# A hybrid attention block on one core: attention units spread over three scheduling periods instead of two

## What is computed

```python
h = modulate(x, g_mix, shift, scale)                 # rmsnorm, then adaLN
proj = h @ w_in                                      # q, k, v of 8 + 8 heads, a gate, forget logits
# stick-breaking heads (8), strict causal
log_beta = log_sigmoid(z); log_keep = where(strict, log_beta - z, 0)
suffix = cumsum(log_keep, reverse=True) - log_keep   # over the keys
w = where(strict, exp(log_beta + suffix), 0);  o_sb = w @ v
# forgetting heads (8), causal; q and k are rms-normed first
z = q @ k.T * scale + f_q - f_keys;  o_fx = softmax(z) @ v
o_sb = rmsnorm(o_sb); o_fx = rmsnorm(o_fx) * sigmoid(gate)
x = x + gate1 * (concat(o_sb, o_fx) @ w_out)
```

## Time and profile before

| | |
|---|---|
| median of 3 runs | 1144.94 us (1144.14 to 1145.12) |
| profiled execution | 1145.88 us |
| its span, first to last instruction | 1144.1 us |
| granted TensorE clock, mean | 0.996 |
| PE busy | 1108.5 us, 97% of the span |
| DVE busy | 596.1 us, 52% |
| ACT busy | 446.4 us, 39% |
| periods 0 to 39 | from 442.9 us to about 725 us of the span |

### The profile page before, as it was taken

The page is one execution under the profiler, slowest core; times in us unless marked ns, Lnnn a source line. Parts: engine busy times, 40 slices in busy tenths (PEclk is TensorE's granted clock), DMA queues, the critical chain, the costliest instruction groups (busy, mean ns, idle before and its releaser), DMA issues.

```text
span 1144.1 us, 14298 instructions
## 1 busy us (share of the span) xinstructions
PE 1108.5 (97%) x5142; PEld 885.2 (77%) x5142; DVE 596.1 (52%) x829; ACT 446.4 (39%) x693; POOL 71.7 (6%) x68
## 2 busy tenths in 40 slices
PE   8999999999999999889999999999999999999997
PEld 5788888888788868678778767778888888878876
DVE  3746464655644556777766677663333333434343
ACT  5522222222222235566776665353222222312312
POOL 1000000000000001000000000000000000225350
PEclk9999999999999999999999999999999999999999
DMA  9755675565573631221212211332333333223221
GB/s 343 212 148 165 195 207 166 165 190 165 166 227 105 193 92 47 80 67 44 73 52 66 65 47 42 89 91 74 92 97 96 97 94 92 74 83 98 96 92 74
DMA packets 169687, 133.32 MB, mean 117 GB/s; under 512 B 5436, under 2 KB 150956, under 8 KB 169644
## 3 DMA queue, kind: packets, MB, share of 16 engines
q1 hardware_dynamic: 168704, 130.60, 38.0%
q0 software_dynamic: 768, 2.10, 0.8%
q10 hardware_dynamic: 172, 0.06, 0.0%
HBM read 128.54 MB, written 2.10 MB: 114 GB/s over the span
## 4 chain that ended last, share of the span: by engine, by line
PE 76%; DVE 12%; ACT 7%; issue 3%; DMA 1%; SPq 0%; DVEq 0%; ACTq 0%
PE bank L694 24%; PE bank L696 24%; PE bank L695 24%; DVE w_lo L1471 2%; DVE tmp_b L1867 2%; DVE pt_lo L1889 1%; PE bank L714 1%; ACT w_hi L1107 1%; ACT tmp_a L1376 1%; DVE tmp_b L1839 1%; ACT tmp_a L1374 1%; ACT tmp_a L1378 1%; DMA w_raw<-in_w_ffn_down_dram 1%; PE bank L1012 1%; DVE tmp_b L1871 1%
## 5 line engine op out<-in xcount | busy, mean ns | idle before, releaser
L1471 DVE TENSOR_TENSOR w_lo<-w_raw,w_hi 128x1024 fp32r<-128x1024 f32 x163 | 216.9, 1332 | 382.6 <-ACT w_hi L1107 382.1
L694 PE MATMUL bank<-h_hi,w_hi 128*128 128x512 f32 x864 | 349.2, 404 | 1.3 <-DVE v_lo L1772 0.3
L695 PE MATMUL bank<-h_lo,w_hi 128*128 128x512 f32 x864 | 342.9, 397 | 0.0
L696 PE MATMUL bank<-h_hi,w_lo 128*128 128x512 f32 x864 | 342.8, 397 | 0.0
L1107 ACT ACTIVATE w_hi<-w_raw 128x1024 fp32r<-128x1024 f32 x163 | 172.3, 1058 | 422.2 <-PE bank L696 402.5
L694 PEld LDWEIGHTS bank<-h_hi,w_hi 128*128 128x128 f32 x864 | 163.2, 189 | 44.9 <-issue 5.5
L695 PEld LDWEIGHTS bank<-h_lo,w_hi 128*128 128x128 f32 x864 | 163.1, 189 | 40.6 <-issue 2.6
L696 PEld LDWEIGHTS bank<-h_hi,w_lo 128*128 128x128 f32 x864 | 163.1, 189 | 39.6
L595 POOL TENSOR_TENSOR w_raw<-w_raw,gate_row 128x1024 f32<-128x1024 f32 (+1 forms) x24 | 54.9, 2287 | 378.9 <-DMA w_raw<-in_w_ffn_down_dram 378.6
L694 PE MATMUL bank<-w_hi,hid_hi 128*128 128x512 f32 x176 | 69.9, 397 | 3.2 <-DVE w_lo L1471 3.2
L694 PE MATMUL bank<-hid_hi,w_hi 128*128 128x512 f32 x176 | 70.1, 398 | 1.0 <-DVE w_lo L1471 1.0
(11 more groups left out here) (215 smaller groups left out, 1342.6 us busy)
## 6 DMA issues: line engine op xcount, KB each, us to landing
w_raw<-in_w_ffn_up_dram SPq DMA_DIRECT2D x88, 512.0 KB, 4.6
ada_w<-in_w_ada_dram SPq DMA_DIRECT2D x56, 512.0 KB, 3.6
w_raw<-in_w_ffn_down_dram SPq DMA_DIRECT2D x36, 512.0 KB, 4.4
w_raw<-in_w_in_dram SPq DMA_DIRECT2D x28, 512.0 KB, 3.7
ada_first<-in_w_ada_dram SPq DMA_DIRECT2D x16, 512.0 KB, 10.9
w_raw<-in_w_out_dram SPq DMA_DIRECT2D x8, 512.0 KB, 3.7
w_raw<-in_w_ffn_down_dram SPq DMA_DIRECT2D x8, 384.0 KB, 4.4
x_nat<-in_x_dram SPq DMA_DIRECT2D x4, 512.0 KB, 5.2
```

The lines of the kernel that those rows point to most:

```text
L694: mm(dst, wh, xh, start=start, stop=False, skip_group_check=skip)
L695: mm(dst, wh, xl, start=False, stop=False, skip_group_check=skip)
L696: return mm(dst, wl, xh, start=False, stop=stop, skip_group_check=skip)
L1471: v.tensor_tensor(w_lo[:, s, :], w_raw[:, r, :], w_hi[:, s, :].bitcast(F32), ALU.subtract)\
```

## The change

The period strings are new, and scores, scan and turn of a unit now stand in three periods: in period p, `T` and `L` are of unit p-2, `U` and `E` of unit p-1, and `S` and `P` of unit p. T stands first, U and L come before P, and the splits (x) stand last. The exp of the last stick-breaking unit is emitted right behind its sum. A stat now needs 10 units of PE work after its square, and a scale 4 after its stat. ACT's abs no longer waits for DVE's relu; it waits for the scores, and relu waits for abs.

```diff
-PERIOD = ("StPaamUdamvbtDTxxLxE", "SmPdaabTvtUtEamxDL")
-LAG_STAT, LAG_BANK, LAG_TILE = 4, 1, 5
+PERIOD = ("TSULPatamEdamvbtDxxx", "TSULPadambvtmtamxD")
+LAG_BANK, LAG_TILE = 1, 5
+LAG = {"stat": 10, "scale": 4}
...
-        if not chains or (chains[0][0][0] == "stat" and not force and spent[0] - since["chain"] < LAG_STAT):
+        if not chains or (not force and spent[0] - since["chain"] < LAG.get(chains[0][0][0], 0)):
             return
...
         before = units[p - 1] if p else None
+        earlier = units[p - 2] if p >= 2 else None
...
-            elif item == "U":
-                emit("sum", j, u)
-            elif item == "E":
-                emit("exp", j, u)
-            elif item == "T" and before:
-                emit("turn", *before)
-            elif item == "L" and before:
-                emit("unload", *before)
+            elif item == "U" and before:
+                emit("sum", *before)
+                if before[0] < SBJ <= j:
+                    emit("exp", *before)
+            elif item == "E" and before:
+                emit("exp", *before)
+            elif item == "T" and earlier:
+                emit("turn", *earlier)
+            elif item == "L" and earlier:
+                emit("unload", *earlier)
...
+    emit("turn", *units[-2])
+    emit("sum", *units[-1])
+    emit("unload", *units[-2])
     emit("turn", *units[-1])
     emit("unload", *units[-1])
...
-                    act.wait_ge(relu_done, unit + 1)
+                    act.wait_ge(s_done, unit + 1)
...
-                    dve.wait_ge(s_done, unit + 1)
+                    if j < SBJ:
+                        dve.wait_ge(abs_done, unit + 1)
+                    else:
+                        dve.wait_ge(s_done, unit + 1)
```

## The result

The changed kernel takes 1192.67 us (median of 4 runs, 1191.32 to 1193.72), the kernel before beside it 1145.03: a ratio of 1.0413 (95% interval 1.0393 to 1.0432), 47.6 us slower where 20.8 were forecast. The profiled execution took 1191.32, its span is 1189.5 us at a mean granted clock of 0.981. PE is busy for 1121.8 us (1108.5 before), DVE 595.3, ACT 447.4: as much as before.

A forecast was written before the change was run, and what follows sets the result against it. PE was taken as the bound, losing time only in waits. New waits of 45.3 us against 21.9 old, plus 3.4 for clock dips, less 6.0 for small waits, made +20.8 us: 1166 us, range 1147 to 1178.

The forecast's parts named there:

- the waits for keys: Forgetting half, periods 29 and 34: scores 6,0 and 7,0 wait 4.6 and 5.8 us for transfers of keys made later.
- the turn of period 21: Start of the forgetting half: the first turn waits 4.2 us for an exp behind decay, split and sum.
- the exp as the largest entry: Sign in PE's waits: exp ahead of a turn comes largest, about 18 us in some eight places.
- the 0.16 that a stop adds: Each PE wait costs about 0.16 us beyond its row, as a matmul shows 0.40 but the next could start 0.235 later.
- Stick-breaking half, 22.2: Stick-breaking half: 22.2 us of new PE waits, from exps late for turns and from other crossings.
- Boundaries, 23.1: Job boundaries of the forgetting half, with period 24: 23.1 us of new PE waits.
- I keep 1.5 of the 7.5: Waits below 1.3 us in nine periods, 7.5 us together, mostly vanish as DVE and ACT catch up: -6.0 us.
- four dips against two: Clock: four new waits are longer than the one that brought a dip, against two dips before: +3.4 us.
- the 21.9 of before: Mixer of the kernel before: PE loses 19.1 us in waits plus 2.8 for some 17 stops.
- The rival with ten dips: Clock rival: every wait near 2 us or above brings a dip, 13.6 us instead of 3.4, so 1176; chance 0.13.
- Relu behind abs costs nothing: Stick-breaking units: relu may follow abs at no cost, since its reader, the scan, is a period later.
- The 2.06 of the earlier trace: DVE stands 2.06 us while ACT makes abs, exp and ln of the unit DVE needs next; spreading was to remove it.

The follow-up runs named there:

- e4: The changed kernel with dummy bf16 matmuls on PE in front of 16 of its 26 waits, order unchanged: 1182.19 us.
- e2: The changed kernel with the old lags, 4 units of PE work from square to stat and none from stat to scale: 1194.25 us.
- e7: The kernel before, with its own strings and lags, and only the swap of abs and relu: 1131.37 us.
- e3: The changed kernel with exp moved ahead of the first tick in stick-breaking periods and the old lags, both together: 1186.57 us.

## Why the prediction was wrong

The direction and the mechanism were right, the size was less than half: the waits for keys, the turn of period 21 and the exp as the largest entry came, but PE idle rose to 51 us where "about 37" was forecast. The forecast's terms go from start to start, so a measured wait counts here with the 0.16 that a stop adds. Its own steps:

- *Stick-breaking half, 22.2.* Close. 19.3 us came in 14 waits, 21.5 with 0.16 for each. PE's idle time by period, measured and forecast: period 2: 1.0 and 1.5; 3: 1.9 and 1.8; 8: 1.9 and 2.4; 11: 2.2 and 2.0; 13: 2.2 and 2.4; 14: 2.5 and 3.0; 16: 2.3 and 3.0; 17: 1.1 and 1.2; 19: 1.9 and 2.6.
- *Boundaries, 23.1.* The first came nearly as written: 3.5 and 4.0 against 4.2 and 4.0; so did period 24 (1.0 and 1.8 against 1.0 and 1.7). The keys waited 3.5 and 3.9 against 4.6 and 5.8, but in front of them, in the same periods, the stats waited 2.3 and 3.8 for the copy of `f_keys`, which the text has as 0.9 each. Together 13.5 against 12.2.
- *The failed step: what was put at nothing.* The text prices the boundaries of the forgetting half and period 24, and leaves the rest of that half at zero. There the turns of units 5,2 and 6,2 waited 2.5 and 1.7 for the forgetting sum, which stands on DVE behind a split, behind ACT, behind a stat; and the projection in period 39 waited 3.5 for `o_lo`. That is 7.7 us.
- *The failed step: "I keep 1.5 of the 7.5", -6.0.* Of the small waits of periods 6 to 24, priced at 5.7 together, 5.1 came, and those of periods 29 and 34 were the 2.3 and 3.8 above. The walk carried the lateness of each queue along already, so nothing was left to take off.
- *The failed step: "four dips against two", +3.4.* The clock cost about three times that. By the forecast's own scale PE's 51.5 us of idle time and 0.16 for each of 26 waits are 55.7; less the 21.9 of before this is +33.8. The spans differ by 45.4, so some 12 remain for the clock, and e4 gives 10.5 back. By the rows of the two stretches the clock is at 1.2 GHz for 2 x (0.03 x 153 + 0.09 x 175) = 41 us, where it was 6; in part of that time PE stood anyway. The rival with ten dips had the clock about right (13.6) and all the rest as too small.
- *"Relu behind abs costs nothing."* True, and not the question. The 2.06 of the earlier trace rows was read as scan behind its own ln, which the spreading would cure; the waits of ACT show just as well an abs behind relu, which the swap cures alone for 14.8 us.

Added up: 24.6 us are missing in the profiled execution (45.4 less 20.8). The clock is 8.2 of them (11.6 instead of 3.4) and waits are 16.4 (55.7 instead of the 39.3 that 22.2, 23.1 and -6.0 make). Of these 6.0 is what was taken off, about 8 what was put at nothing, and some 2 the boundaries themselves.

Busy time by stretch of the changed kernel in windows of 4 us around four of its waits (1.87 in period 8, 2.16 in 11, 1.87 in 16, 1.87 in 19):

```profile
494.20:498.20 4.00, 2.13 (x15) 1.40 (x14) 0.63 (x1) 3.36 (x7) 0.00 (x0) 1.00 0.00 0
498.20:502.20 4.00, 4.00 (x35) 4.00 (x35) 3.97 (x8) 1.72 (x3) 0.00 (x0) 1.00 0.50 131
...
524.00:528.00 4.00, 2.04 (x8) 1.66 (x9) 2.82 (x4) 2.93 (x5) 0.00 (x0) 0.91 0.01 4
528.00:532.00 4.00, 3.94 (x17) 3.13 (x16) 1.92 (x4) 0.63 (x2) 0.00 (x0) 0.67 0.50 131
...
562.00:566.00 4.00, 2.13 (x14) 1.37 (x13) 0.64 (x1) 3.32 (x6) 0.00 (x0) 1.00 0.00 0
566.00:570.00 4.00, 3.58 (x16) 2.60 (x15) 3.97 (x6) 1.72 (x3) 0.00 (x0) 1.00 0.45 131
...
585.00:589.00 4.00, 2.13 (x11) 1.28 (x10) 3.90 (x8) 3.07 (x7) 0.00 (x0) 0.96 0.50 133
589.00:593.00 4.00, 4.00 (x13) 3.14 (x12) 3.05 (x6) 2.66 (x5) 0.00 (x0) 0.61 0.00 0
```

Columns as in the earlier trace rows. Behind a dip PE is shown busy for all of the 4.00 us, at 0.61 with 13 matmuls: busy time at the lower level (1.2 GHz) looks like work and is half lost. The page "TensorE: Matmul & The Clock Gate" of the Trainium skill, section "Why this matters for your kernels", says that gaps between bursts bring the clock down. The traces agree, for gaps of 1.9 us too, but not each time: of the three of 1.87 us one brought a dip and two did not.

**What the 47.6 us are made of.** The swap alone gives about 15; everything else of the change costs 61.3 on top of it (1192.67 less 1131.37). The new lags have no part in that sum: with the old ones it is 62.9 (e2, 1194.25). So it is the new order. By halves, against the 134.2 and 133.0 of e7, it costs 19 us in the stick-breaking half and 42 in the forgetting half (153.2 and 175.4), with the old lags 29 and 32 (163.0 and 164.7). In that, the clock is about 10 and the length of the splits in line about 11 (these overlap). The rest hangs on no single link that was tried: moving the exp, the scan, the unload, the splits or the turn, or giving a buffer more, made it equal or slower in eleven of twelve tries; the one that was faster (e3) gave 6 us. What the traces show is that ACT and DVE wait for each other and for PE in more places than before (ACT 15.1 us for the turn and 48.0 for DVE's `prep`, DVE 21.0 for the high parts of splits), with scan and exp in line behind. That these waits are what makes PE wait is read from the chain at period 21 and from the sums; no run shows it for the whole. Whether another order with three periods could beat e7 stays open; none of those tried that compute all came within 50 us of it.

## What to carry to other kernels

Ask for the waits of the engines off the bound, in both directions, before an order is redone: a pair such as 36.0 us of DVE for ACT and 27.1 us of ACT for DVE pointed here at one needless order between two operations that both only read the scores, and swapping these two was worth 14.8 us where no rescheduling gained anything. In a list that no engine may leave, a longer distance between producer and consumer moves the consumer behind other work that waits for the bound, so count what it will stand behind, not only how early its input is. Price the clock by the number of waits, not by the longest alone: here 26 of them cost about 10 us by the clock, where four dips at the longest had been priced at 3.4 more than before. And end a stretch at the same point of the work, not at a round time, when its length is compared.

## What was not expected of the hardware

Three waits of PE of the same length, 1.87 us, in stretches with the same busy time (2.13 of 4 us), ended differently: the granted clock stayed at 1.00 around two of them and went to 0.61 behind the third. And matmuls that compute nothing, put into waits, gave back 10.5 us of 47.6 by the clock alone.
